# Expert stage of an encoder layer: another order of weight splits behind the loop, and of activations within each tile

## What is computed

```
g_idx = argmax(softmax(t @ w_group + b_group))          # one of 4 groups
top_v, top_i = top_k(softmax(e_logits of that group), 2) # two of its 4 experts
for e in range(16):
    gu = t @ w_gate_up[e]                                # 1024 -> 512
    y = (silu(gu[:, :256]) * gu[:, 256:]) @ w_down[e]    # 256 -> 1024
    out = out + combine[:, e:e + 1] * y
```

## Time and profile before

| what | us |
|---|---|
| median of 3 runs (643.83 to 644.86) | 644.76 |
| the profiled execution | 644.76 |
| its span | 642.9 |

### The profile page before, as it was taken

The page is one execution under the profiler, slowest core; times in us unless marked ns, Lnnn a source line. Parts: engine busy times, 40 slices in busy tenths (PEclk is TensorE's granted clock), DMA queues, the critical chain, the costliest instruction groups (busy, mean ns, idle before and its releaser), DMA issues.

```text
span 642.9 us, 8490 instructions
## 1 busy us (share of the span) xinstructions
PE 613.2 (95%) x3084; PEld 498.5 (78%) x3084; DVE 410.7 (64%) x756; ACT 338.2 (53%) x607; POOL 63.0 (10%) x78
## 2 busy tenths in 40 slices
PE   5999999999999999999999998899999999789997
PEld 4878888888888777887888876678877778678885
DVE  6322265343542565557786987889988886856672
ACT  7741222322223575556555666789988886931211
POOL 0000000000000000110111114212212211110000
PEclk9999999999999999999999999989999999979999
DMA  8913305120212430110105447999999999533511
GB/s 350 372 52 149 98 2 193 33 82 18 98 34 65 172 133 0 66 34 35 66 34 195 166 152 260 385 410 411 410 406 401 394 351 344 196 118 115 173 40 66
DMA packets 34650, 113.74 MB, mean 177 GB/s; under 512 B 5384, under 2 KB 6024, under 8 KB 34608
## 3 DMA queue, kind: packets, MB, share of 16 engines
q1 hardware_dynamic: 28752, 99.99, 41.9%
q0 software_dynamic: 4896, 12.59, 5.2%
q10 hardware_dynamic: 960, 0.61, 0.4%
HBM read 103.70 MB, written 14.71 MB: 184 GB/s over the span
## 4 chain that ended last, share of the span: by engine, by line
PE 73%; DMA 16%; DVE 5%; ACT 3%; issue 2%; SPq 0%; POOL 0%; POOLq 0%; DVEq 0%; ACTq 0%
PE bank L474 20%; PE bank L476 19%; PE bank L475 19%; DMA w_raw_more<-in_w_moe 10%; PE bank L1773 5%; PE bank L1800 3%; DMA w_raw<-in_w_moe 3%; PE bank L1819 3%; PE bank L1781 2%; DVE w_split L453 2%; ACT w_split L447 1%; PE bank L1928 1%; DMA pick<-moe_rows 1%; ACT s L878 1%; DMA moe_x<-h_rows,slot_token 1%
## 5 line engine op out<-in xcount | busy, mean ns | idle before, releaser
L474 PE MATMUL bank<-w_split,h_T_prompt 128*128 128x512 f32 x192 | 77.4, 403 | 6.9 <-DVE w_split L1228 6.9
L476 PE MATMUL bank<-w_split,h_T_prompt 128*128 128x512 f32 x192 | 75.6, 394 | 0.0
L475 PE MATMUL bank<-w_split,h_T_prompt 128*128 128x512 f32 x192 | 75.6, 394 | 0.0
L469 DVE TENSOR_TENSOR w_split<-w_raw,w_split 128x1024 fp32r<-128x1024 f32 x33 | 40.2, 1221 | 42.1 <-ACT w_split L464 42.0
L453 DVE TENSOR_TENSOR w_split<-w_raw,w_split 128x1024 fp32r<-128x1024 f32 x48 | 57.1, 1220 | 7.0 <-ACT w_split L447 6.9
L453 DVE TENSOR_TENSOR w_split<-w_raw_more,w_split 128x1024 fp32r<-128x1024 f32 x44 | 52.6, 1220 | 9.9 <-ACT w_split L447 9.7
L474 PE MATMUL bank<-w_split,moe_xT 128*128 128x512 f32 x120 | 49.5, 413 | 7.2 <-DVE moe_xT L1617 7.1
L447 ACT ACTIVATE w_split<-w_raw 128x1024 fp32r<-128x1024 f32 x48 | 49.4, 1062 | 6.5 <-DMA w_raw<-in_w_moe 5.7
L447 ACT ACTIVATE w_split<-w_raw_more 128x1024 fp32r<-128x1024 f32 x44 | 45.7, 1061 | 9.2 <-DMA w_raw_more<-in_w_moe 8.5
L474 PEld LDWEIGHTS bank<-w_split,h_T_prompt 128*128 128x128 f32 x192 | 36.6, 191 | 15.1 <-DVE w_split L1228 6.9
L476 PE MATMUL bank<-w_split,moe_xT 128*128 128x512 f32 x120 | 47.8, 398 | 0.0
(11 more groups left out here) (275 smaller groups left out, 1346.3 us busy)
## 6 DMA issues: line engine op xcount, KB each, us to landing
w_raw<-in_w_moe SPq DMA_DIRECT2D x50, 512.0 KB, 13.2
w_raw_more<-in_w_moe SPq DMA_DIRECT2D x42, 512.0 KB, 16.2
w_raw<-in_w_in SPq DMA_DIRECT2D x24, 512.0 KB, 5.4
pick<-moe_rows SPq DMA_DIRECT2D x10, 512.0 KB, 4.5
w_raw<-in_w_out SPq DMA_DIRECT2D x8, 512.0 KB, 3.5
toep<-bias_table SPq DMA_DIRECT2D x4, 896.0 KB, 7.6
x_row<-in_x SPq DMA_DIRECT2D x6, 512.0 KB, 9.6
x_again<-in_x SPq DMA_DIRECT2D x6, 512.0 KB, 3.3
```

The costliest lines, as they stand in the source:

```text
L469: nc.vector.tensor_tensor(W[:, u % WS, 1], raw(u)[0], f(W[:, u % WS, 0]), ALU.subtract).then_inc(lo_done, 1)
L474: nc.tensor.matmul(out, hi, whi, start=first, stop=False)
L475: nc.tensor.matmul(out, lo, whi, start=False, stop=False)
L476: return nc.tensor.matmul(out, hi, wlo, start=False, stop=last)
```

## The change

Four lists are written in another order.

- SP: behind the loop it first loads (3,4) and (3,5) (when the last set's down units are split), then, once tile 1's gate/up is done, (2,4) and (2,5), then the gain row, then everything from tile 4 on in the order of the list. Before, (4,0) and (4,1) came first, (3,4) and (3,5) behind (4,3), and the gain row ahead of (8,0).
- ACT and DVE: the split of (1,4) and (1,5) comes first behind the loop, and tile 2's four gate/up units next, with the silu (product) of tile 1 and the tokens of tile 2 behind them. In tiles 3 to 14 the activations of the tile before are taken ahead of the split of (t+1,2) instead of behind it.
- TensorE: `turn_x(2)` moves from the middle of tile 1's gate/up to its end, and loses its wait for the loop's last token copy.

```diff
--- SP
-            for j in range(2):
-                moe_unit((4, j))
+            for j in range(4, 6):
+                sp.wait_ge(lp_lo, n * 4 + (j + 1))
+                moe_unit((3, j))
             sp.wait_ge(pe_gu, 1)
             for j in range(4, 6):
                 moe_unit((2, j))
-            for j in range(2, 4):
-                moe_unit((4, j))
-            for j in range(4, 6):
-                sp.wait_ge(lp_lo, n * 4 + (j + 1))
-                moe_unit((3, j))
+            sp.dma_start(gain[:], gains[2]).then_inc(gain_ld, 16)
             for u in STREAM:
-                if u == (8, 0):
-                    sp.dma_start(gain[:], gains[2]).then_inc(gain_ld, 16)
-                if u[0] > 4 or u in ((4, 4), (4, 5)):
+                if u[0] > 3:
                     moe_unit(u)
--- ACT (DVE has the same with moe_lo, xT_lo, act_mul, loop_lo, actT_lo)
-            for j in range(3):
-                moe_hi((2, j))
-            xT_hi(2)
-            moe_hi((2, 3))
-            silu(1)
             for j in range(4, 6):
                 loop_hi(n, j)
-            actT_hi(1)
-            for j in range(3):
-                moe_hi((3, j), n)
-            for t in range(2, LAST + 1):
-                if t > 2:
-                    if t < LAST:
-                        moe_hi((t + 1, 2))
+            moe_hi((2, 0))
+            moe_hi((2, 1))
+            for t in range(1, LAST + 1):
+                if t > 1:
                     actT_hi(t - 1)
                 if t < LAST:
+                    moe_hi((t + 1, 2), n if t == 2 else None)
                     moe_hi((t + 1, 3), n if t == 2 else None)
-                moe_hi((t, 4))
+                if t > 1:
+                    moe_hi((t, 4))
                 silu(t)
...
--- PE
                 if t > 1:
                     turn_act(t - 1)
-                else:
-                    pe.wait_ge(lp_dxt, n * 2 + 2)
-                    turn_x(2)
                 gate_up(t, range(2, 4))
-                if 1 < t < LAST:
+                if t < LAST:
                     turn_x(t + 1)
```

More of the change, by code:

```diff
@@ L1156, in _ @@
                     xT_hi(t + 1)
-                moe_hi((t, 5))
+                if t > 1:
+                    moe_hi((t, 5))
                 if t + 2 <= LAST:
-                    moe_hi((t + 2, 0))
-                    moe_hi((t + 2, 1))
-                y_out(t - 1)
+                    moe_hi((t + 2, 0), n if t == 1 else None)
+                    moe_hi((t + 2, 1), n if t == 1 else None)
+                if t > 1:
+                    y_out(t - 1)
             actT_hi(LAST)
@@ L1672, in _ @@
                     loop_lo(i * 4 + (j + 5), j)
+            for j in range(4, 6):
+                loop_lo(n * 4 + (j + 1), j)
             moe_lo((2, 0))
             moe_lo((2, 1))
[L1676 to L1688, removed]
+            for t in range(1, LAST + 1):
+                if t > 1:
                     actT_lo(t - 1)
                 if t < LAST:
+                    moe_lo((t + 1, 2))
                     moe_lo((t + 1, 3))
-                moe_lo((t, 4))
+                if t > 1:
+                    moe_lo((t, 4))
                 act_mul(t)
@@ L1695, in _ @@
                     xT_lo(t + 1)
-                moe_lo((t, 5))
+                if t > 1:
+                    moe_lo((t, 5))
                 if t + 2 <= LAST:
```

## The result

| | us | ratio to before, 95% interval |
|---|---|---|
| before | 644.67 | |
| with the change, first six timed runs | 648.38 (647.27 to 651.72) | 1.0067 [1.0044, 1.0090] |
| the same kernel again (10 runs) | 646.69 | 1.0028 [1.0012, 1.0045] |
| the same kernel a third time (12 runs) | 646.39 | 1.0023 [1.0010, 1.0035] |

The change makes the kernel slower, as forecast. The forecast was 647.4, plus 2.6 us. The three measurements say plus 3.7, 1.9 and 1.6 us.

What follows compares the result with a forecast made beforehand. The weight stream was taken to bound the expert stage to 535 us. Tile 1's turn at 417.7 plus 13 x 9.72 puts tile 14's at 544.1, 2.6 us late, so 644.76 becomes 647.4 us; range 644.6 to 649.8.

Steps and rivals of the forecast that it cites:

- The bound before: Expert stage: to 535 us the full weight stream sets the pace; the engines have some 0.7 us a tile in hand.
- First term: Hand-over from the loop: tile 2's gate/up starts at 412.85 instead of 405.80 us, so tile 1's turn comes at 415.7.
- Second term: Low TensorE clock behind the 7 us hand-over idle slows tile 2's first matmuls by 2.0 us; tile 1's turn at 417.7.
- Third term: Order within tiles 3 to 14: the engines' path from turn to turn grows from 9.32 to 9.72 us a tile.
- The sum: Tile 1's turn plus 13 steps: 417.7 + 13 x 9.72 = 544.1 for tile 14's turn, 2.6 us later than 541.46.
- rival (a): Expert stage: the weight stream hides the late engines; 644.8 to 645.6 us, chance 0.27.
- What costs nothing: SP's new load order and the earlier 512 KB gain row: the weight stream does not run dry, its bytes unchanged.
- Rival (b): Final stage: a shifted idle puts less work under the low clock, up to 3 us back; 642 to 644, chance 0.07.
- Rival (c): Hand-over: unit (1,5) lands late, up to 652 us; chance 0.06 together with an emptying stream.

Runs made afterwards that it cites:

- before_delay: The kernel before with 13 spare matmuls (3.0 us) put on TensorE in tile 4; 644.65 us, ratio 0.9997.
- both_fill: The changed kernel with 29 spare matmuls filling TensorE's 7 us idle ahead of tile 2's gate/up; 645.40 us, ratio 1.0008 to before.
- half_order: The changed kernel with the old place of the activations' split in tiles 3 to 8 only; 644.87 us, ratio 1.0003 to before.
- before_tail: The kernel before with TensorE's idle ahead of the final stage's first gate filled by spare matmuls; 642.39 us, ratio 0.9955.
- handover_only: The changed kernel with the old ACT and DVE order inside tiles 3 to 14; 644.46 us, ratio 0.9996 to before.
- order_only: The kernel before with only the new ACT and DVE order inside tiles 3 to 14; 644.97 us, ratio 1.0005.
- sp_only: The kernel before with only the new order of loads on SP; 645.78 us, ratio 1.0013.
- both_tail: The changed kernel with the idle ahead of the final stage's first gate filled by spare matmuls; 645.67 us, ratio 1.0002 to before.
- both_fill_tail: The changed kernel with spare matmuls both ahead of tile 2's gate/up and ahead of the final stage; 643.49 us, ratio 0.9976 to before.

## Why the prediction was right, point by point

- **The bound before** was read rightly. The steps of the kernel before are held by the stream from the step to tile 8 on (9.32 to 9.37 us up to tile 7, then 9.7 to 10.6), and before_delay shows the reserve by giving 3 us back.
- **First term** (hand-over): forecast 412.85 for tile 2's start, 14.78 behind the first load. Measured 412.12 - 397.29 = 14.83, behind an idle of 6.95 us where 7 were forecast. The rows of the landing, 3.7 and 4.6 us, held in this trace. Over the nine traces with this hand-over the start lies 14.3 to 14.9 us behind the first load.
- **Second term** (clock): 2.0 forecast, with 2.3 as the bound. Measured 1.8 to 2.4 from the start of tile 2's gate/up to the turn, 1.85 in the first trace. With both_fill 0.7 us of the cost is left, and its interval includes none. The Trainium skill's advice not to fit the slow matmuls (TensorE: Matmul & The Clock Gate, Part 1: The HAM clock gate) would have left this term out. The traces agree that their number varies, from 9 to 12 of tile 2's first twelve, but here the term was most of what went over the reserve.
- **Third term** (path inside a tile): 9.72 forecast, 9.73 measured in all three traces. The chain shows the same parts.
- **The sum**: tile 14's turn 2.6 us late by forecast, 2.7 by the first pair of traces. (The lag of 4.9 us at tile 5, named under rival (a), is 4.7 by the sum's own terms, and 4.7 in the traces.) **One mis-sized part** is the base. The single trace of before has the smallest distance of all kernels that the stream holds: 143.4, against 143.9 to 144.4 in half_order, before_delay, before_tail, handover_only and order_only. Against their middle, 144.2, the change is 1.5 to 2.0 us late, and the timed runs of the second and third measurement say 1.9 and 1.6. The stream-held turn was taken for a fixed number, and it moves by 1 us between executions. **The other** is the end, which was taken to be as now. In the traces of the changed kernel it is 1.4 to 2.0 us shorter than in that of before, with the shorter low stretch. That the three medians lie on both sides of 647.4 is therefore in part luck.
- **What costs nothing**: right for the changed kernel, but not for the reason that I gave alone. The trace of sp_only shows that the order on SP needs the new order on ACT and DVE.
- **Rival (a)**, the stream hides it, was near: with either half alone it is what happens. With the clock held up the engines reach tile 14 just when the stream would let them. **Rival (b)** was half right: the profiled execution came out at 644.75 with a shorter low stretch in the final stage, and by their clock so may about half of the later timed runs, but it did not make the change faster. **Rival (c)** did not happen.

Open: why the first six timed runs lay 3.7 us over before, and the later 22 only 1.6 to 1.9. The mean clock does not account for it. Four of the six are at 0.984 to 0.989 and took 648.2 to 651.7 us, two are at 0.991 and took 647.27 and 647.92; the four lie 0.7 to 4.2 us over the median of the later group with such clocks, the two 2.2 to 2.8 over theirs, while the profiled execution of that set, at 0.991, took 644.75. No trace of the six exists.

## What to carry to other kernels

A stage held by a full weight stream has a reserve on its engines: the time by which the engines alone would be ahead of the stream, here 5.8 us at tile 14 (0.7 us a tile while the stream holds them). Edits that each spend a part of it measure as free, and together they need not be; so size the reserve, and add up what has been spent. In a hand-written order on an engine that executes in sequence, put the split that needs nothing new into the wait for another engine, not behind it; that one place was 0.4 us a tile here. And where a single trace stands for the base, ask how much its anchor moves between executions.

## What the runs showed of the hardware

- In seven traces TensorE is idle for 6.4 to 7.0 us at the hand-over. The 1.2 GHz level begins before the idle is over and lasts 6.8 us (10.2 in both_tail), and the first twelve matmuls behind it take 1.8 to 2.4 us longer. With 29 spare matmuls in the idle the clock stays at 1.00 in both traces (both_fill, both_fill_tail).
- Ahead of the final stage the same cure was worth 2.4 us of 644.8 in the kernel before (before_tail), more than the change costs in its second and third measurement, but only 0.7 to 1.0 us in the changed kernel (both_tail).
- A stream at a DMA share of 0.99 does not tell whether it is the bound. With 0.99 in both, a delay of 3 us on TensorE cost -0.1 us in one order and 2.85 us in the other.
- Loads on one queue land in the order of issue (in before those issued at 403.3, 403.7 and 406.0 land at 412.9, 414.2 and 415.5), each about as late as there is work ahead of it: 3.7 us behind an almost empty queue, 9.5 to 13 us at the hand-over the earlier trace rows, 17.6 us in the full stream. With work in the queue a pause of the issuer does not show: in the changed kernel SP issues nothing from 410.9 to 413.2 us, and the rate stays at 418 to 420 GB/s from 410 to 416. In sp_only, where SP waits until 409.3 with less queued, it falls to 266.
